# Who sums the squares for three RMS norms: GpSimd adding tiles, or TensorE accumulating them

## What is computed

```
h = concatenate([meta, x])
h = h + 0.5 * rmsnorm(swiglu(rmsnorm(h, n[0]), ffn1_wi, ffn1_wo), n[1])
h = h + rmsnorm(hybrid_mixer(rmsnorm(h, n[2]), ...), n[3])
h = h + 0.5 * rmsnorm(swiglu(rmsnorm(h, n[4]), ffn2_wi, ffn2_wo), n[5])
rmsnorm(x, g) = x * rsqrt(mean(x * x) + EPS) * g
```

## Time and profile before

| | |
|---|---|
| median of three runs | 1113.67 us |
| the profiled execution | 1111.69 us |
| its span, first to last instruction | 1109.9 us |
| TensorE matmul busy | 1029.5 us, 93% of the span |
| TensorE weight loads busy | 1000.7 us, 90% |
| VectorE busy | 648.1 us, 58% |
| ScalarE busy | 478.9 us, 43% |
| GpSimd busy | 744.8 us, 67% |
| chain that ended last, by engine | TensorE 79%, VectorE 14%, ScalarE 4%, GpSimd 2% |
| mean granted TensorE clock | 0.953 of full speed |

### The profile page before, as it was taken

The page is one execution under the profiler, slowest core; times in us unless marked ns, Lnnn a source line. Parts: engine busy times, 40 slices in busy tenths (PEclk is TensorE's granted clock), DMA queues, the critical chain, the costliest instruction groups (busy, mean ns, idle before and its releaser), DMA issues.

```text
span 1109.9 us, 21393 instructions
## 1 busy us (share of the span) xinstructions
PE 1029.5 (93%) x8164; PEld 1000.7 (90%) x8164; DVE 648.1 (58%) x1028; ACT 478.9 (43%) x706; POOL 744.8 (67%) x348
## 2 busy tenths in 40 slices
PE   4799999998989999997989999989999969999996
PEld 4699999998979999997789888989999959999995
DVE  6333995546865565446794644437556676665454
ACT  5444223545354445434446623433235445445441
POOL 3685655555858787996566723556548839888993
PEclk9899999999989999998898988989999969999998
DMA  7454333442635555664244112433225615556661
GB/s 256 134 173 151 115 115 119 130 133 83 195 92 182 185 162 177 175 176 146 96 151 134 58 38 86 133 106 115 98 94 147 210 62 173 186 180 182 187 192 54
DMA packets 47864, 154.87 MB, mean 140 GB/s; under 512 B 5980, under 2 KB 11108, under 8 KB 47604
## 3 DMA queue, kind: packets, MB, share of 16 engines
q1 hardware_dynamic: 45648, 151.31, 43.7%
q10 hardware_dynamic: 2152, 2.65, 0.7%
HBM read 151.85 MB, written 2.10 MB: 139 GB/s over the span
## 4 chain that ended last, share of the span: by engine, by line
PE 79%; DVE 14%; ACT 4%; POOL 2%; issue 1%; DMA 0%; DVEq 0%; SPq 0%; ACTq 0%
PE panel L1504 62%; PE panel L1535 4%; PE aux L1602 2%; DVE qkv L1239 1%; DVE xl L971 1%; PE aux L1791 1%; POOL wlo L569 1%; DVE qkv L1230 1%; DVE qkv L1234 1%; DVE h L986 1%; DVE tmp L981 1%; DVE sq L1014 1%; PE aux L1828 1%; PE aux L1867 1%; PE aux L1876 1%
## 5 line engine op out<-in xcount | busy, mean ns | idle before, releaser
L569 POOL TENSOR_TENSOR wlo<-raw,whi 128x1024 fp32r<-128x1024 f32 x284 | 700.9, 2487 | 308.6 <-ACT whi L662 308.5
L1504 PE MATMUL panel<-xh,whi 128*128 128x256 f32 (+1 forms) x1504 | 444.0, 295 | 24.6 <-DVE xl L971 18.5
L1504 PE MATMUL panel<-xl,whi 128*128 128x256 f32 (+1 forms) x1504 | 435.1, 289 | 0.0
L1504 PE MATMUL panel<-xh,wlo 128*128 128x256 f32 (+1 forms) x1504 | 434.2, 289 | 0.0
L662 ACT ACTIVATE whi<-raw 128x1024 fp32r<-128x1024 f32 x284 | 294.2, 1052 | 187.7 <-PE panel L1504 152.0
L1504 PEld LDWEIGHTS panel<-xh,whi 128*128 128x128 f32 x1504 | 291.7, 194 | 33.4 <-DVE xl L971 14.2
L1504 PEld LDWEIGHTS panel<-xh,wlo 128*128 128x128 f32 x1504 | 291.7, 194 | 0.0
L1504 PEld LDWEIGHTS panel<-xl,whi 128*128 128x128 f32 x1504 | 290.9, 193 | 0.6
L1504 PE MATMUL panel<-hh,whi 128*128 128x272 f32 (+1 forms) x352 | 100.1, 284 | 0.0
L1504 PE MATMUL panel<-hh,wlo 128*128 128x272 f32 (+1 forms) x352 | 99.9, 284 | 0.0
L1504 PE MATMUL panel<-hl,whi 128*128 128x272 f32 (+1 forms) x352 | 99.8, 284 | 0.0
(11 more groups left out here) (292 smaller groups left out, 1616.6 us busy)
## 6 DMA issues: line engine op xcount, KB each, us to landing
raw<-in_panels SPq DMA_DIRECT2D x236, 512.0 KB, 3.5
raw<-in_down SPq DMA_DIRECT2D x32, 448.0 KB, 3.3
raw<-in_down SPq DMA_DIRECT2D x16, 512.0 KB, 3.5
memx<-in_mem SPq DMA_DIRECT2D x1, 1024.0 KB, 5.5
h<-in_x SPq DMA_DIRECT2D x1, 1024.0 KB, 8.4
spill<-h ACTq DMA_DIRECT2D x1, 1024.0 KB, 6.2
h<-spill ACTq DMA_DIRECT2D x1, 1024.0 KB, 7.4
out<-h SPq DMA_DIRECT2D x2, 512.0 KB, 2.9
```

Source lines behind the costliest of these rows:

```text
L569: nc.gpsimd.tensor_tensor(wlo[:, slot, :], raw[:, slot, :], whi[:, slot, :].bitcast(f32), ALU.subtract).then_inc(lo_ready, 1)
L1504: ins = M(bank[:, 0:w], wt[:, slot, P * t:P * t + P], x[:, kk, c0:c0 + w], start=first and m == 0 and n == 0, stop=last and m == len(pairs ...
```

## The change

At norms 3, 5 and 7 GpSimd no longer adds. TensorE multiplies the ones by the squares of each tile, right behind this tile's three products of the first output, and accumulates the eight results in the `aux` bank. It opens that bank ahead of the first output instead of behind it. The count that the untouched norms wait for in `summed` is adapted.

```diff
-            def sum_squares(n):
-                for kk in range(1, KT):
-                    pool.wait_ge(squared, 8 * SPLIT[n] + kk + 1)
-                    ins = nc.gpsimd.tensor_tensor(sq[:, 0, 0:W[n]], sq[:, 0, 0:W[n]], sq[:, kk, 0:W[n]], ALU.add)
-                    if kk < KT - 1:
-                        order(ins)
-                ins.then_inc(summed, 1)
...
             ahead(WOUT_P + 15)
-            sum_squares(3)
             loop(UP + 24)
-            sum_squares(5)
...
             ahead(OUT2_P + 7)
-            sum_squares(7)
...
-                pe.wait_ge(summed, n + 1)
+                pe.wait_ge(summed, n + 1 if n < 2 else n // 2 + 2)
...
+            def first_output(o, p, w, n):
+
+                bank, use = aux("stat", n)
+                open_output(o, p)
+                aux_open(use)
+                for kk in range(KT):
+                    pe.wait_ge(split_low, 8 * SPLIT[n] + kk + 1)
+                    ins = products(pb[o % 4], p % RING, [(kk, kk)], xh, xl, 0, w, kk == 0, kk == KT - 1)
+                    pe.wait_ge(squared, 8 * SPLIT[n] + kk + 1)
+                    total = M(bank[:, 0:w], ones[:], sq[:, kk, 0:w], start=kk == 0, stop=kk == KT - 1)
+                ins.then_inc(passed, 1)
+                total.then_inc(aux_full, 1)
...
-                output(first_o, first_p, xh, xl, w, each=tiles_split(norm))
-                norm_stat(norm)
+                first_output(first_o, first_p, w, norm)
...
-                if kind in ("qkv", "fourier_in", "sconv"):
-                    output(o, p, xh, xl, LEN, each=tiles_split(5) if step == ("qkv", 0) else None)
-                    if step == ("qkv", 0):
-                        norm_stat(5)
+                if step == ("qkv", 0):
+                    first_output(o, p, LEN, 5)
+                elif kind in ("qkv", "fourier_in", "sconv"):
+                    output(o, p, xh, xl, LEN)
```

## The result

The changed kernel takes 1101.17 us (median of four runs, 1099.59 to 1101.46) beside 1113.36 us for the kernel before: ratio 0.9878, 95% interval 0.9865 to 0.9892. It is faster by 12.2 us by the medians and by 13.6 us by the ratio. From 1113.67 us, the median that the forecast starts from, it is 12.5 us.

What follows compares the result with a forecast made beforehand. At the three norms VectorE's links, slowed by GpSimd's additions, were taken as the bound, not TensorE. Winning 1.9 + 3.8 + 3.0 = 8.7 us at norms 3, 5 and 7 gave 1105.0 us, range 1102 to 1111.

Steps and rivals of the forecast that it cites:

- VectorE's links: At norms 3, 5 and 7, six links each shorten once GpSimd stops adding: 3.1, 3.1 and 2.9 us, 9.1 together.
- What it adds: Seven more ones matmuls per norm on TensorE; a tile then costs 0.83 us at full and 1.59 at half clock.
- The clock: TensorE's clock falls around each stage's start and returns 3.7 to 6.1 us after unbroken work begins.
- The ends of 3.7 and 6.1 us: Two delays, read elsewhere in the trace, from the start of unbroken TensorE work until full clock is back.
- the middle: At norm 7, 3.0 us won, between 3.6 and 2.4 for the early and late return of the clock.
- What follows: Behind each stage the gain is kept; the fourth panel's chain has no slack, and later outputs win nothing more.
- Rival 1: Clock stays low for the whole first output: 3 to 6.4 us lost, about 1118 us; chance 0.07.
- Rival 2: Clock returns late at all three norms, or gain is partly lost behind norm 5: about 1109.5 us; chance 0.16.
- Rival 3: VectorE's links are long for another reason; only the tail shortens, 2.3 us in all, 1111.4 us; chance 0.05.
- Rival 4: The change doesn't do what it says, as when TensorE's order breaks weight preloading: about 1113 us; chance 0.02.
- How the numbers follow: Step from 8.7 us won in the three stages to the whole kernel's median: 1113.67 - 8.7 = 1105.0 us.
- some tenths of spread: Allowance between runs, added to 11.1 us won, that set the range's low end at 1102 us.

Runs made afterwards that it cites:

- e3: Changed kernel with GpSimd still adding pairs of square tiles, at the old places, into a scratch tile nobody reads: 1110.12 us, ratio 0.9969 to before.
- e2: Kernel before without GpSimd's additions; the ones are multiplied by the first tile alone, so the three norms' sums are incomplete: 1102.36 us, ratio 0.9904.
- e7: Changed kernel with all eight ones matmuls together behind the last tile's products instead of one behind each tile: 1113.27 us, ratio 0.9980 to before.
- e16: Changed kernel without an edit, measured a third time: 1101.12 us, ratio 0.9908 to the kernel before.
- e6: Kernel before with the change at norm 5 alone; norms 3 and 7 keep GpSimd's sums: 1108.99 us, ratio 0.9959 to before.
- e5: Changed kernel without an edit, measured again: 1103.79 us, ratio 0.9905 to the kernel before.
- e8: Kernel before with dummy ones matmuls ahead of the three first outputs and of norm 6's ones: 1111.94 us, ratio 0.9983 to before.
- e4: Changed kernel with 6 or 8 dummy ones matmuls ahead of the three first outputs and 6 ahead of norm 6's ones: 1100.67 us, ratio 0.9897 to before.
- e12: The same kernel as e4, changed kernel plus dummy ones matmuls, measured again: 1101.26 us, ratio 0.9893 to the kernel before.
- e11: Changed kernel with squares and ones rounded to fp32r, so that a ones matmul is one pass: 1102.60 us, ratio 0.9899 to before.

## Why the prediction was right or wrong

**VectorE's links: right.** No link of lines 959, 969, 974 and 1175 at the three norms is above 0.51 us, and the last split starts 5.5, 7.3 and 7.0 us after the first (forecast: 5.7, 7.4, 7.1). In the three stages VectorE's busy time fell by 9.0 us, where 9.1 were forecast. e3 brings the links back and loses 8 of the 11 us; e2 shows them short without TensorE's part. The reading of the earlier trace rows, an exact overlap, carried this. The Trainium skill's page "SBUF — State Buffer", section "SBUF: two separate sides", says of the pair of ports that VectorE and GpSimd share that the later one waits for the whole of the other's instruction. e3 agrees: the split that began 0.10 us behind an addition of 0.79 us ended 0.30 us after it and took 0.99 us, not 0.49.

**What it adds: right.** A tile takes 0.84 us at full and 1.59 at half clock (forecast 0.83 and 1.59). e7 shows what the same eight matmuls cost where nothing hides them: 4.83 us.

**The clock: right in kind, mis-sized at two places.** The ends of 3.7 and 6.1 us after unbroken work held in this profile: 3.7, 4.9 and 5.5 were measured. At norm 5 I had taken 3.7. At norm 7 I had taken the middle, 4.9.

| | forecast, us won | measured in the profile | what differs |
|---|---|---|---|
| norm 3 | 1.9 | 1.94 | nothing |
| norm 5 | 3.8 | 3.13 | clock back after 4.9 us, not 3.7 |
| norm 7 | 3.0 | 2.65 | clock back after 5.5 us, not 4.9 |
| sum | 8.7 | 7.7 | 8.7 in the mean of three profiles |

From the first product until TensorE was free for the second output it took, counted as in the prediction, 8.3, 9.1 and 9.0 us (8.4, 8.4, 8.6 forecast). At norm 3 the clock doesn't fall in every execution (e16), which gives 3.5 us instead of 1.9. I had no such case. So the 8.7 us in the mean of three profiles meet the forecast partly by luck: the case that it describes, a fall at each norm, gave 7.7 and 8.2.

**What follows: right in the main.** The stretches behind norms 3 and 7 kept their 198.2 and 186.5 us, so the gain of the stages stays. e6 is less clear: its whole agrees with 3.8 us kept, its profile doesn't show it. The fourth panel has no slack. In after TensorE waited for its low part (timeline; in brackets the wait):

```profile
908.29 0.39 PE L1492 MATMUL panel<-xh,whi 128*128 128x256 f32 x1 [0.19 <-POOL wlo L569]
```

**The rivals.** Rival 1 didn't occur. Rival 2 (2 to 6 us won) didn't either: the clock was later than taken at two norms, but the stages won 7.7 us. Rival 3 is excluded by the links of after and by e3. Rival 4 is excluded by the chain.

**How the numbers follow: this step failed.** The forecast is 3.8 us above the measured median. By the pooled medians this splits into 0.6 us because 1113.67 lies above 1113.04, 0.4 because the first four runs of after lie below 1101.6, and 2.7 that the stages don't hold (11.4 less 8.7). Beside the profile of before, the three profiles of the changed kernel won 3.0, 1.3 and 1.9 us outside the stages, 2.1 in the mean; the remaining 0.6 us lie in executions without a profile. Two terms of the range were wrong, both put at nothing or nearly so. First, "some tenths of spread" at the low end: executions of the changed kernel differ by 5 us, and the three runs shown, 1112.43 to 1115.43, already said 3. Second, everything outside the three stages was held fixed at a gain of 0, whereas it was 1.3 to 3.0 us. It is partly luck on which side of the bound a batch falls: with e5's six executions (median 1103.79) the forecast would have held, with e16's (1101.12) not. A low end 3 us lower would have been right: 11.1 us won and 3 us for the rest is 1099.6. Why the untouched stretches got shorter stays open; the time at half clock in the mixer goes with it.

## What to carry to other kernels

Look at the length of an engine's links in the chain before its share: the same instruction at 0.41 and 0.91 us, with another engine's instruction beside each long one, tells that work on an idle engine is slowing the busy one. Work that TensorE takes over costs little where it fills gaps between tiles, and here it brought the clock back earlier; the same work in a row behind them cost most or all of the gain (e7). And a change that shifts everything behind it by several microseconds also changes where the clock falls: give the range 1 to 3 us for that, and compare several executions before a difference of 2 us is explained.

## What the runs showed of the hardware

- The granted clock fell in the middle of a stage though TensorE had been kept busy ahead of it (e8: 314.4, 526.1 and 905.0), while its busy share there was 0.16 to 0.76. With dummies and with the ones between the tiles it did not fall at the three norms (e4, e12; 0.92 us busy in the window shown).
- Less time at half clock didn't always mean less time in all. e8 had 20.5 us less of it than before and is 1.6 us quicker; e12 had 20.5 less than after and is as fast. In e8 the clock was up where VectorE set the pace, and the stages kept their length. In e12 the stages were 3.3 us shorter and the start and the mixer longer.
- A VectorE operation with two inputs in SBUF took 0.90 to 0.94 us in place of 0.41 (128 x 272, fp32) where a GpSimd addition of the same kind was under way (before and e3).
- A plain fp32 matmul of 128 x 128 by 272 columns costs 0.46 us at full and 0.91 at half clock, recorded as two passes; in fp32r it is one pass of 0.12 (e11).
